# No gated value split ahead in the last up turn: all 22 in the tiles of the sums of h

## What is computed

```python
def _swiglu(h, w13, w2):
    g, u = jnp.split(h @ w13, 2, axis=-1)
    return (jax.nn.silu(g) * u) @ w2
```

## Time and profile before

| what | value |
|---|---|
| time, median of three | 3205.27 us |
| the three executions | 3204.94, 3205.27 and 3210.66 us |
| profiled execution | 3210.57 us |
| its span | 3208.7 us |
| PE busy | 2992.0 us, 93% |
| DVE busy | 2209.9 us, 69% |
| ACT busy | 1384.4 us, 43% |
| POOL busy | 1590.5 us, 50% |
| mean granted clock of PE | 0.979 |

### The profile page before, as it was taken

The page is one execution under the profiler, slowest core; times in us unless marked ns, Lnnn a source line. Parts: engine busy times, 40 slices in busy tenths (PEclk is TensorE's granted clock), DMA queues, the critical chain, the costliest instruction groups (busy, mean ns, idle before and its releaser), DMA issues. The chain is left out here.

```text
span 3208.7 us, 57420 instructions
## 1 busy us (share of the span) xinstructions
PE 2992.0 (93%) x22801; PEld 2554.6 (80%) x22801; DVE 2209.9 (69%) x3864; ACT 1384.4 (43%) x2651; POOL 1590.5 (50%) x1197
## 2 busy tenths in 40 slices
PE   5999999889999899999889999999888889989998
PEld 4899876679987899877789987987666666778887
DVE  6899488689965899652689965536677764774443
ACT  3555235445533455234454523226544434435343
POOL 3676442357644676443467644224667760143332
PEclk8999999999999999999999999999899999999999
DMA  6565532236553565532234543213222233222222
GB/s 203 166 195 176 158 85 66 59 114 209 172 178 91 160 195 162 154 90 72 71 119 152 153 145 128 75 55 111 65 58 58 56 107 70 95 77 72 79 66 59
DMA packets 641458, 367.05 MB, mean 114 GB/s; under 512 B 107902, under 2 KB 634132, under 8 KB 640688
## 3 DMA queue, kind: packets, MB, share of 16 engines
q1 hardware_dynamic: 633216, 351.57, 37.4%
q10 hardware_dynamic: 6640, 10.49, 1.1%
q0 software_dynamic: 1344, 1.44, 0.2%
HBM read 334.27 MB, written 24.97 MB: 112 GB/s over the span
## 5 line engine op out<-in xcount | busy, mean ns | idle before, releaser
L270 POOL TENSOR_TENSOR w_lo<-w_raw,w_hi 128x1024 fp32r<-128x1024 f32 (+1 forms) x181 | 432.9, 2393 | 820.9 <-ACT w_hi L262 755.1
L262 ACT ACTIVATE w_hi<-w_raw 128x1024 fp32r<-128x1024 f32 (+1 forms) x172 | 175.2, 1019 | 378.9 <-PE acc L335 264.6
L1265 PE MATMUL scaled<-h_terms,h 128*128 128x256 f32 x1856 | 260.5, 283 | 0.0
L1265 PEld LDWEIGHTS scaled<-h_terms,h 128*128 128x128 f32 x1856 | 239.4, 192 | 0.0
L957 DVE SCALAR_TENSOR_TENSOR ada_part<-ada_raw,c_act,ada_part 128x256 f32<-128x256 f32 x432 | 210.6, 487 | 16.1
L335 PE MATMUL acc<-h_terms,w_hi 128*128 128x512 f32 x560 | 209.7, 393 | 3.3 <-POOL w_lo L270 3.3
L335 PE MATMUL acc<-hid,w_hi 128*128 128x512 f32 x528 | 205.6, 389 | 0.0
L335 PE MATMUL lat<-h,w_slots 128*128 128x512 f32 x672 | 199.6, 396 | 4.5 <-ACT plain L3945 4.0
L335 PE MATMUL acc<-h_terms,w_lo 128*128 128x512 f32 x496 | 193.4, 390 | 0.0
L648 DVE TENSOR_TENSOR scaled<-z,x 128x512 f32<-128x512 f32 x36 | 41.9, 1164 | 184.7 <-ACT z L589 184.7
L1113 POOL TENSOR_TENSOR h<-z,h 128x512 fp32r<-128x512 f32 x80 | 108.0, 1350 | 113.0 <-ACT h L1144 112.6
(11 more groups left out here) (785 smaller groups left out, 8897.4 us busy)
## 6 DMA issues: line engine op xcount, KB each, us to landing
w_raw<-in_ffn_w SPq DMA_DIRECT2D x240, 512.0 KB, 4.2
ada_raw<-in_ada_w SPq DMA_DIRECT2D x88, 1024.0 KB, 5.7
w_raw<-in_od_w_in SPq DMA_DIRECT2D x32, 512.0 KB, 4.1
w_raw<-in_ffn_w SPq DMA_DIRECT2D x32, 384.0 KB, 3.5
w_raw<-in_ev_w_in SPq DMA_DIRECT2D x22, 512.0 KB, 3.9
image<-inverse_wait SPq DMA_DIRECT2D x144, 64.0 KB, 2.1
first_ada<-in_ada_w SPq DMA_DIRECT2D x8, 1024.0 KB, 12.5
w_raw<-in_ab_w_in SPq DMA_DIRECT2D x16, 512.0 KB, 4.0
```

The lines of the kernel that those rows point to most:

```text
L262: act.activation(K.w_hi[:, first % SPLIT, 0:tiles, :], K.raw[:, first % RAW, 0:tiles, :], ACT.Copy).then_inc(K.hi_ready, 1)
L270: pool.tensor_tensor(K.w_lo[:, first % SPLIT, 0:tiles, :], K.raw[:, first % RAW, 0:tiles, :], K.w_hi[:, first % SPLIT, 0:tiles, :].bitcast ...
L1265: pe.matmul(out_of[p], hi_of(t, p)[:, k, :], moving[p][:, part, k, :], start=k == 0 and part == HI, stop=False)
```

## The change

`EARLY` goes from 4 to 0. All numbers that were written out for EARLY = 4 are written as sums with EARLY. Place and condition of every value follow from it: values 0 to 3 now wait for `left_done`, 4 to 11 for `right_done`, 12 to 21 for `turn_done`, and four places in the lo half of h are added to the list.

```diff
-EARLY = 4
+EARLY = 0
...
-        hid_place = [*range(20, 28), *range(16, 20), *range(4, 8), 28, 29]
+        hid_place = [*range(20, 28), *range(16, 20), *range(4, 8), 28, 29, *range(12, 16)]
         hid_hi = lambda j: K.h_first[:, 1, j, :] if j < EARLY else terms[:, hid_place[j - EARLY], :]
...
                         if j < EARLY:
                             act.wait_ge(S.turn_done, count - 1)
-                        elif j < 8:
+                        elif j < EARLY + 4:
                             act.wait_ge(S.left_done, count)
-                        elif j < 16:
+                        elif j < EARLY + 12:
                             act.wait_ge(S.right_done, count)
                         else:
                             act.wait_ge(S.turn_done, count)
...
-                        hidden_hi(0, 2)
+                        hidden_hi(0, EARLY // 2)
...
-                        hidden_hi(2, EARLY)
+                        hidden_hi(EARLY // 2, EARLY)
                         down_hi(0)
                         down_hi(1)
...
-                hidden_hi(EARLY, 16)
+                hidden_hi(EARLY, EARLY + 12)
                 silu(FB - 1)
                 split_hi(act, K, down, 0, 0, 2, tiles[2])
-                hidden_hi(16, FB)
+                hidden_hi(EARLY + 12, FB)
```

## The result

The changed kernel takes 3214.65 us (median of 14 executions, 3212.22 to 3216.81); the kernel before takes 3209.03 us over 14 executions of its own, three of which are those shown ahead. The profiled execution has 3215.79 us, its span 3213.9 us (before 3208.7), and PE is busy for 2995.5 us, 93%. So the total came as forecast. Its parts did so only up to PE's read of the ada sum, with one step wrong before it (chunk 3) and something that the sum had no term for behind it (the granted clock).

A forecast was written before the change was run, and what follows sets the result against it. The prediction took PE, busy 93% of the span, as the bound, so edits count through its waits. It added 2 x 0.6 + 2 x 2.0 = +5.2 us to 3205.27, forecasting 3210.5 us, range 3206 to 3215.5.

The forecast's parts named there:

- The edits ahead of the seam gain nothing: First seam, turn 21: removing four ACT copies and four DVE subtractions gains nothing, since PE waited for none of it.
- Value 0 in time, lead of 0.4 us at value 12: First seam, block 0: value 0 ready without a PE wait, margin 0.5 us; value 12's lead over PE is 0.4 us.
- Rival 5: Block 0: PE also stands at value 0; first two seams lose 0.5 to 1 us more, +6.5 in all, chance 0.08.
- Chunk 2 free of its hold, value 12 held: First seam: POOL's chunk 2 takes 1.84 us, removing PE's 1.66 us wait; value 12 is held, costing 1.05 us.
- Chunk 3 gets in at DVE's next start (+0.6 in each of the first two): First two seams: POOL's chunk 3 enters at DVE's next start, holding value 21; block 1 starts 0.6 us later.
- rival 1: POOL is held for DVE's whole stream: -0.15 us in each of the first two seams, +3.7 in all, chance 0.15.
- The ada read 2.0 us later in the last two: Third and fourth seam, block 1: four more DVE subtractions and shifted port blocks delay the ada sum, +2.0 us each.
- Nothing later takes it up: Behind the seams: no later slack absorbs the +5.2 us; each down part has only one PE wait.
- The sum: All four seams: 2 x 0.6 + 2 x 2.0 = +5.2 us.
- the 0.2% that the prediction took for the least that shows: Whole kernel: a measurement can't tell less than about 0.2%, 6.4 us, from no change; "same" had chance 0.66.
- Rivals 3 and 4: 3: DVE's 1.3 us lead hides held subtractions, -3.9 us, chance 0.06; 4: later phases absorb cost, 0 to +1, chance 0.09.

The follow-up runs named there:

- the ada read later: PE's read of the ada sum behind each block's second chunk instead of its first: in the changed kernel 3206.14 us, in the kernel before 3201.58 us.
- the filling: Changed kernel with eight unused products of constants ahead of PE's ada read in block 1 of the third and fourth seam: 3212.37 us, ratio 1.0011.
- the product later in the changed kernel: Changed kernel with DVE's product of turn 21 behind value 15 and ACT's copies 12 to 15 ahead of chunk 2's split: 3215.44 us, ratio 1.0018.
- the two edits together: Kernel before with DVE's product of turn 21 behind value 15 and PE's ada read one chunk later: 3198.13 us, ratio 0.9969.
- the control with the filling: Kernel before with the same eight unused products of constants ahead of PE's ada read, third and fourth seam: 3210.98 us, ratio 1.0007.

## Why the prediction was right, and where it wasn't

*The edits ahead of the seam gain nothing.* Right: block 0 starts without a wait in all four.

*Value 0 in time, lead of 0.4 us at value 12.* Right. Value 0 starts at 299.26 in the rows above, PE has no wait until value 12. Rival 5 doesn't occur.

*Chunk 2 free of its hold, value 12 held.* Right in mechanism at all four seams: 1.85 us on POOL, 1.93 on DVE, a wait of 0.76 us and a slow first matmul. The two cost the forecast 1.05 us: the tile of value 12 starts 0.92 us late (309.80 against 308.20 + 0.68 from the tile ahead of it), and the next follows after 0.81 instead of 0.68. In the second seam the wait is 1.02, since the split of chunk 2 starts 0.28 us later there; that came in all four profiles with this order (the changed kernel twice, the ada read later, the filling) and isn't explained.

*Chunk 3 gets in at DVE's next start (+0.6 in each of the first two).* This step failed. It was held to the end of the stream in all four seams, which is what rival 1 said, with a chance of 0.15; so block 1 came 0.08 us earlier in the first seam and 0.2 later in the second. I chose by majority among the requests that I saw; what decides it is not settled. A request 0.48 us ahead of DVE's next start got in before, one 0.43 ahead did not here. Nor does the lead decide: with two values ahead one of 0.56 us did not get in (first seam), and with the product later in the changed kernel one of 0.05 us did (third seam, POOL 2.37 us). What held in all twelve profiles is that POOL's chunk 2 gets through beside DVE's instruction that reads PSUM (L1401), wherever that one runs at or behind the request.

*The ada read 2.0 us later in the last two.* Right to 0.02 us, and half of it with half of the values. "Nothing later takes it up" was right too, but I hadn't asked whether something later makes it worse. PE's idle time in these two parts went from one wait to three, and the granted clock fell behind the third: +1.6 and +3.2 us in the one profile, +3.2 and +3.2 in the other. The sum put this at nothing.

*The sum.* Forecast +0.6, +0.6, +2.0, +2.0. The down parts show 0.0, +0.3, +3.6, +5.2, in all +9.1 us, and the rest of the profiled pair is 3.9 us shorter, so the spans differ by 5.2. The rest moves by as much between executions of one kernel: the part between the first and second seam has 460.65 us in one profile of the changed kernel and 462.17 in the other, that between the third and fourth 434.40 and 432.66. Stretches at the lower clock come and go there. Windows of 10 us before, in the changed kernel and in the changed kernel again:

```profile
587.00:597.00 10.00, 7.30 (x25) 5.51 (x25) 7.14 (x10) 4.22 (x6) 5.15 (x2) 0.83 0.21 60
587.00:597.00 10.00, 7.34 (x32) 5.62 (x31) 7.08 (x7) 4.22 (x6) 5.18 (x2) 1.00 0.25 71
587.00:597.00 10.00, 7.34 (x25) 5.59 (x26) 7.14 (x9) 4.22 (x6) 5.16 (x2) 0.83 0.21 61
```

The part between the first two seams has 461.85 to 462.97 us in the eight profiles with this stretch of 3.4 us, of either kernel, and 460.52 to 460.65 in the four without. One near 1500 us goes in the same way with the part between the third and the fourth: 434.16 to 434.55 us in seven, 432.33 to 432.81 in five. So of the 3.9 us, 1.4 go with the stretch near 593 us, which the profile before has and the changed one has not. 2.35 lie behind the fourth down part, and what makes these isn't shown.

That the profiled pair differs by the forecast 5.2 is therefore luck in part, a balance of misses: -0.9 us at chunk 3 (0.3 for 1.2), +4.8 of clock in the seams and -3.9 elsewhere. Without the clock the down parts give +4.3 us, nearer to the 3.7 of rival 1 than to 5.2. The medians of the two occasions, +5.6 and +4.4, each with some 3 us either way, can't tell these sums apart. They do tell the change from none: 14 executions of each kernel leave 5.6 us between 3.9 and 9.0, so the 0.2% that the prediction took for the least that shows was too coarse.

*Rivals 3 and 4* fall with the waits at value 12 and the read at 24.60.

## What to carry to other kernels

Work that is taken out of a slack turn and put behind it costs what the stream that it joins costs, even if the engine that bounds the kernel has no wait in either place; look for the next join of that stream (here block 1's weights and the ada sum). Where two engines exclude each other, count not only durations but who asks when: an instruction that leaves the shared resource free, moved by a few places to where the other engine asks, took 1.9 us off each of two seams at no cost. And a small wait that has slack behind it, such as the ada read, is cheaper to move than to shorten: the two edits together gave 0.9969.

## What the runs showed of the hardware

A POOL subtraction of SBUF operands was passed over at seven starts of DVE in a row (6.02 us against 1.84). It was so in the first two seams in all four profiles of kernels that keep this order there (the two of the kernel before, the ada read later, the control with the filling), while in the last two seams of the same profiles it gets in at the next start (2.21 to 2.28 us). The Trainium skill (SBUF — State Buffer, section on the two separate sides) gives the port to whoever starts first, for its whole instruction. The trace agrees that the other is blocked meanwhile (value 12 takes 1.93 us instead of 0.68). But the end of one instruction did not hand the port to the engine that waited, seven times in a row.

The granted clock of PE fell to its lower level behind three waits of 0.76, 0.66 and 2.0 us in 25 us, in both profiles of the changed kernel and at both places, and stayed there for 3.4 to 6.8 us. It did not fall behind a single wait of 2.0 us, nor behind the same three when the last was filled with 1.95 us of idle products. Behind waits of 0.3, 1.6 and 1.3 us (the product later in the changed kernel) it fell at both places, for 3.4 us. With two waits of 1.3 and 1.4 us (two values ahead) it fell in the fourth seam and not in the third. Each 3.4 us at the lower level costs some 1.6 us (3.62 - 2.0).
